# Adaptive-norm columns: four chunks before the first matmul instead of eight, and a gate that goes through DRAM

## The chip, the cores and the metric

One core of one Trainium2 chip runs the whole kernel in one launch. The metric is the device time in microseconds (us). The kernel before took 2486.54 us (median of 3 runs, 2486.16 to 2488.39). Engines: TensorE (PE) multiplies, VectorE (DVE) and ScalarE (ACT) work on vectors, SyncE (SP) issues all DMAs of the kernel before, and GpSimd (POOL) does nothing in it but four memsets.

## The reference

A sequence of 256 tokens of width 1024 (x, float32) goes through four layers of three sublayers: a gated feed-forward network (FFN), a mixer, and another FFN. Each sublayer is wrapped in an adaptive norm, whose shift, scale and gate come from one conditioning vector c:

```
mod = (silu(c) @ ada_w[l] + ada_b[l]).reshape(B, 3, 3, 1, D)      # 9 x 1024 numbers a layer
h   = rmsnorm(x, norm_g[l, j]) * (1 + mod[:, j, 1]) + mod[:, j, 0]
x   = x + 0.5 * (1 + mod[:, 0, 2]) * swiglu(h, wi, wo)            # FFN; in layers 2, 3 the gate has no "1 +"
x   = x + (1 + mod[:, 1, 2]) * mixer(h)
```

FFN: 1024 to 2 x 2816 to 1024. Mixers: a gated linear recurrence (hgrn) in layer 0, differential attention (diff) in layer 1, sparse attention beside a gated MLP (nsa) in layers 2 and 3. A last rmsnorm ends it. All in float32.

## The kernel before, in words

Twelve phases (l, j), l = 0..3 and j = 0..2, run one after the other. Weights come in pieces of 1 MB (128 x 2048), through a ring of three buffers `raw`. SP issues a piece when the piece three places earlier has been cut. "Cutting" splits it in a high and a low part, so that three float32r products make one float32 product: ACT copies the high part into `wH` (L461), DVE subtracts to get `wL` (L786), PE multiplies (L1371, L1373, L1375). Each engine's order is written out by hand, with counted semaphores; nothing is planned by a scheduler.

An FFN phase takes 33 pieces, in eleven turns: PE runs the up projection of 256 channels into `GU` (two pieces), ACT and DVE make silu(gate)*up, PE turns it (L1421), ACT and DVE split it (L524, L887), PE adds the down projection into `PY`.

The adaptive-norm numbers `mod` (288 columns of 128) are dot products on DVE. A chunk is four columns: two transfers of 1 MB of the transposed `ada_w` and four products of 128 x 1024 with `cond` (L793), then a small store (L813). Columns are in the order shift, scale, gate, eight each; so a phase's shift and scale are four chunks, and its gate two more. Of layer 0, eight chunks come ahead of everything (`start_products`, through a ring of five 1 MB buffers, L366), and ten in the turns of phase (0, 0); the later layers' chunks go one to a turn in FFN phases: 8 turns in each (l, 2), 10 in each (l, 0) (`ada_turns`).

At the boundary between phases (`boundary` on DVE, `norm` on ACT, `norm_and_first` on PE):

- DVE `columns` (L823 to L837) makes the gate column `gcol` and spreads it into `sh` (L833), and makes `scl`. PE `gate_broadcast` (L1378 to L1383) multiplies `sh` by the identity (16 matmuls) into `TM`, and ACT copies that to `gB` [128, 1024] (L511). `gB` is used at the next boundary, when DVE multiplies the phase's output with it (L841) and adds it to x (L845).
- For each of the two token tiles: ACT squares x (L473), DVE and ACT make the root (L818, L475, L821), DVE scales the identity (L861), PE multiplies x with it into `PY`, transposed (`turn_x`, L1389), DVE and ACT apply scale and shift (L868, L495), ACT and DVE split the result (L490, L874), PE starts the first products.
- In the very first boundary x is read straight after it has landed, and ACT does one more cut (the third piece) between the root of tile 0 and the split.

SP's order at the start: `cond`, `vec`, the identity, the first ten 1 MB transfers of `ada_w`, x, the other six, two weight pieces, six transfers of late constants (`late_constants`, L379 to L387, used first in hgrn), then the loop of phase (0, 0).

Of the kernel before, what the change touches and what calls it, by code (L numbers as in the profile page):

```python
# [25 lines left out]
P = 128  # L26
# [90 lines left out]
def build(nc, T, out, upto=99):  # L117

    with ExitStack() as ctx:
# [145 lines left out]
        s_gp = sem("s_gp")  # L265
# [50 lines left out]
        ADA_FIRST, ADA_REST = 8, 10  # L316
# [6 lines left out]
        def ada_turns(l, j):  # L323

            if j == 0:
                return l, ADA_FIRST, ADA_REST
            return (l + 1, 0, ADA_FIRST) if l + 1 < 4 else (l, 0, 0)

# [5 lines left out]
        def _(sp):  # L334
# [18 lines left out]
            def load_mixer(w, pieces):  # L353

                at = 0
                for k0, lo, width in pieces:
                    load(w[:, at:at + 4 * width], 4 * width)
                    at += 4 * width

            def load_start(c, q):  # L360

                n = t.next("start")
                slot = n % START_RING
                if n > START_RING:
                    sp.wait_ge(s_startfree, n - START_RING)
                sp.dma_start(start_[slot], T["ada_t"][0, 2 * c + q]).then_inc(s_start[slot], 16)  # L366
# [5 lines left out]
            def load_ada(l, c, q):  # L372
                v = T["ada_t"][l].rearrange("(c q) p n -> q p c n", q=2)
# [15 lines left out]
            def ffn(l, j):  # L389
                load_up(l, j, 0, 0)  # L390
                load_up(l, j, 0, 1)
                if (l, j) == (0, 0):
                    late_constants()
                if (l, j) == (1, 2):
                    sp.wait_ge(s_adafree, ADA_RING + 2 * (2 * ADA_REST + ADA_FIRST))
                    load_cond(1)
                la, c0, turns = ada_turns(l, j)

                def loop(first, count, with_ada):
                    with sp.Fori(0, count) as i:  # L400
                        t.enter(i, [(s_split, 3), ("piece", 3), (s_adafree, 2 * with_ada), ("ada", 2 * with_ada)])
                        load_up(l, j, first + i, 0)
                        if with_ada and (l, j) == (2, 2):
                            sp.wait_ge(s_x, NT * (3 * l + 2))
                        if with_ada:
                            load_ada(la, c0 + i, 0)
                        load_up(l, j, first + i, 1)
                        if with_ada:
                            load_ada(la, c0 + i, 1)
# [13 lines left out]
            for c in range(ADA_FIRST):  # L423
                for q in range(2):
                    load_start(c, q)
                if c == 4:
                    sp.dma_start(x[:, :, :], T["x"][0].rearrange("(t p) d -> p t d", p=P)).then_inc(s_in, 16)
            for l, j in PHASES:
                if j != 1:
                    ffn(l, j)  # L430
                elif l < 2:
                    load_mixer(T["ab"[l] + "_w"], (PIECES_A, PIECES_B)[l])
# [20 lines left out]
        def _(act):  # L453
# [23 lines left out]
            def norm(l, j):  # L477
# [48 lines left out]
            def ffn(l, j):  # L526
                norm(l, j)
                silu_gate()
                if (l, j) == (1, 2):
                    condition()  # L530

                def loop(count):
                    with act.Fori(0, count) as i:
                        t.enter(i, [("piece", 3), (s_eaten, 3), ("done", 3), (s_ht, 1)] + [(s, 32) for s in s_raw])
                        cut()
                        hidden_high()
                        cut()
# [5 lines left out]
                _, _, turns = ada_turns(l, j)  # L543
# [211 lines left out]
            condition()  # L755

# [17 lines left out]
        def _(dve):  # L774
# [14 lines left out]
            def products(l, q, piece, free):  # L789
# [7 lines left out]
            def start_products(q):  # L797
# [3 lines left out]
                products(0, q, start_[slot], s_startfree)  # L801

            def ada_products(l, q):
# [3 lines left out]
                products(l, q, ada[:, slot, :], s_adafree)  # L807

            def ada_store(l, c, free, count):

                dve.wait_ge(free, count)
                at = l * MODS + 4 * c
# [10 lines left out]
            def columns(l, j):  # L823

                m = (3 * l + j) * 3 * ND
                g = 2 * ND + (3 * l + j) * ND
                factor = 0.5 if j != 1 else 1.0
                gate = mod[:, m + 2 * ND:m + 3 * ND]
                if l < 2:
                    chained(dve.tensor_scalar(gcol[:, :], gate, 1.0, factor, ALU.add, ALU.mult))  # L830
                else:
                    chained(dve.tensor_scalar(gcol[:, :], gate, factor, None, ALU.mult))
                dve.tensor_copy(shf.rearrange("p (d n) -> p d n", n=P),  # L833
                                bc(gcol[:, :].unsqueeze(2), [P, ND, P])).then_inc(s_gcol, 1)
                dve.scalar_tensor_tensor(scl[:, :], mod[:, m + ND:m + 2 * ND], 1.0, cols[:, g:g + ND],
                                         ALU.add, ALU.mult).then_inc(s_scl, 1)
                dve.wait_ge(s_scl, t.next(s_scl))  # L837
# [8 lines left out]

            def boundary(l, j, pieces):
# [5 lines left out]
                if pieces:  # L853
                    dve.wait_ge(s_gb, t.next(s_gb))
# [3 lines left out]
                for i in range(NT):  # L858
                    toks = slice(i * P, (i + 1) * P)
                    root(i)  # L860
                    dve.tensor_scalar(diag[:, i, :], ident, rstd[:, i:i + 1], None, ALU.mult).then_inc(s_xn, 1)  # L861
# [28 lines left out]
            def ffn(l, j):  # L890
# [3 lines left out]
                la, c0, turns = ada_turns(l, j)  # L894

                def loop(count, with_ada):
                    with dve.Fori(0, count) as i:
# [5 lines left out]
                        if with_ada:  # L903
                            ada_products(la, 0)
                            ada_products(la, 1)
# [5 lines left out]
                        if with_ada:  # L911
                            ada_store(la, c0 + i, s_adafree, t.next(s_adafree, 0))
                    t.leave(count)

                if turns:
                    loop(turns, 1)
# [67 lines left out]
            def hgrn():  # L984
# [4 lines left out]
                for grp in range(2):  # L989
# [17 lines left out]
                    for n in range(9):  # L1007
# [5 lines left out]
                        if grp == 0 and n < 6 or grp == 1 and n == 7:  # L1013
                            cut()
                    select(8)
                    if grp == 1:
# [7 lines left out]
                                      ).then_inc(s_on, 1)  # L1024
                    d = slice(4 * grp, 4 * grp + 4)
# [302 lines left out]
            for c in range(ADA_FIRST):  # L1328
                start_products(0)
                start_products(1)  # L1330
                ada_store(0, c, s_startfree, 2 * c + 2)
            pieces = 0
            for n, (l, j) in enumerate(PHASES):
                if n == 0 or PHASES[n - 1][1] == 1:
                    cut()
                boundary(l, j, pieces)
                if j != 1:
# [8 lines left out]
            dve.wait_ge(s_gb, t.next(s_gb))  # L1346
# [6 lines left out]
            if len(PHASES) == 12:  # L1353
# [3 lines left out]
                for i in range(NT):  # L1357
                    root(i)
                    dve.scalar_tensor_tensor(x[:, i, :], x[:, i, :], rstd[:, i:i + 1], fg, ALU.mult, ALU.mult
                                             ).then_inc(s_x, 1)  # L1360


        @block.tensor
        def _(pe):
# [13 lines left out]
            def gate_broadcast():  # L1378
                pe.wait_ge(s_gcol, t.next(s_gcol))
                for d in range(ND):  # L1380
                    ins = pe.matmul(TM[:, d // 4, (d % 4) * P:(d % 4 + 1) * P], shf[:, d * P:(d + 1) * P], ident,
                                    start=True, stop=True)
                ins.then_inc(s_gp, 1)  # L1383

# [8 lines left out]
            def norm_and_first():  # L1393


                gate_broadcast()
# [15 lines left out]
                pe.wait_ge(s_gb, t.next(s_gb))  # L1412
# [459 lines left out]
```

## Time and profile before

| | before |
|---|---|
| median of 3 runs | 2486.54 us |
| the profiled execution | 2491.22 us, span 2489.6 us |
| PE / DVE / ACT busy | 91% / 66% / 44% |
| mean granted PE clock | 0.956 of full |
| DMA | 531.30 MB, 213 GB/s over the span |
| chain that ended last | PE 81%, DVE 9%, ACT 5%, issue 2%, DMA 2% |

The chain is followed back from the last instruction to whatever released each step. PE's share of it says that most of the time is matmuls back to back; the slice row of the page shows PE idle in the first slice (62 us) and the granted clock (PEclk) under full in some slices. A clock of 1.00 is 2.4 GHz, 0.5 is 1.2 GHz. A stretch that holds both levels shows a mean.

### The profile page before, as it was taken

Reading aid. Unit: us, or ns where it says so; the run is one execution under the profiler, and the core shown is the slowest. Engines: PE = TensorE matmul, PEld = TensorE weight load, DVE = VectorE, ACT = ScalarE, POOL = GpSimd, SP = SyncE. Lnnn points to the kernel's source line nnn. Section 1 sums busy time; section 2 is a strip of 40 time slices with the busy share of each in tenths; the row PEclk is TensorE's granted clock in tenths of the full one; section 3 lists DMA queues with packets and bytes.
Section 4 is the critical chain, followed back from the end, with each engine's and each line's share of the span. In section 5 each row is a group of like instructions: output and inputs, shape, how many; then the busy total and the mean of one; then the engine's idle time right before and its main releaser. Section 6 shows DMA issues by size and latency. Waiting matters only on the chain.

```text
span 2489.6 us, 30572 instructions
## 1 busy us (share of the span) xinstructions
PE 2273.3 (91%) x11004; PEld 1900.7 (76%) x11004; DVE 1654.5 (66%) x2245; ACT 1097.5 (44%) x1225; POOL 0.2 (0%) x4
## 2 busy tenths in 40 slices
PE   0999995899999997899999998999999999899998
PEld 0788884688788875788788787778878888777886
DVE  7677576677577776587577754468767776446444
ACT  1444543343444355434443444544344445464433
POOL 0000000000000000000000000000000000000000
PEclk9999997899999997999999997899999999799999
DMA  9687430388578731387588732348857883223553
GB/s 382 265 319 279 161 136 0 136 310 311 204 265 312 273 143 70 129 335 281 193 311 308 284 128 85 102 162 316 298 203 274 320 310 128 85 102 126 179 202 110
DMA packets 126426, 531.30 MB, mean 213 GB/s; under 512 B 14736, under 2 KB 15504, under 8 KB 107280
## 3 DMA queue, kind: packets, MB, share of 16 engines
q1 hardware_dynamic: 126352, 530.30, 58.8%
q8 instruction: 48, 0.79, 0.1%
q14 instruction: 26, 0.21, 0.0%
HBM read 529.19 MB, written 1.05 MB: 213 GB/s over the span
## 4 chain that ended last, share of the span: by engine, by line
PE 81%; DVE 9%; ACT 5%; issue 2%; DMA 2%; SPq 1%; DVEq 0%; ACTq 0%
PE GU L1371 14%; PE GU L1375 14%; PE GU L1373 14%; PE PY L1371 9%; PE PY L1373 9%; PE PY L1375 9%; DVE wL L786 2%; ACT wH L461 2%; PE PY L1389 2%; PE TM L1421 1%; DMA M<-in_ada_t 1%; PE GU L1758 1%; PE PY L1668 1%; DVE M L793 1%; DVE x L845 1%
## 5 line engine op out<-in xcount | busy, mean ns | idle before, releaser
L786 DVE TENSOR_TENSOR wL<-raw,wH 128x2048 fp32r<-128x2048 f32 x352 | 794.6, 2279 | 280.9 <-ACT wH L461 279.3
L461 ACT ACTIVATE wH<-raw 128x2048 fp32r<-128x2048 f32 x352 | 659.6, 1899 | 203.4 <-PE PY L1375 102.4
L1371 PE MATMUL GU<-wH,xH 128*128 128x512 f32 (+1 forms) x1600 | 635.2, 397 | 31.6 <-DVE xL L874 13.2
L1375 PE MATMUL GU<-wH,xL 128*128 128x512 f32 (+1 forms) x1600 | 623.8, 390 | 0.0
L1373 PE MATMUL GU<-wL,xH 128*128 128x512 f32 (+1 forms) x1600 | 623.3, 390 | 0.0
L1371 PEld LDWEIGHTS GU<-wH,xH 128*128 128x128 f32 x1600 | 302.8, 189 | 97.1 <-issue 32.6
L524 ACT ACTIVATE hH<-TM 128x512 fp32r<-128x512 f32 x88 | 52.7, 598 | 691.5 <-PE TM L1421 691.5
L1375 PEld LDWEIGHTS GU<-wH,xL 128*128 128x128 f32 x1600 | 302.3, 189 | 63.7
L1373 PEld LDWEIGHTS GU<-wL,xH 128*128 128x128 f32 x1600 | 303.0, 189 | 58.5
L793 DVE CUSTOM_DVE_ANT_0 ada<-ada,cond 128x1024 f32<-128x1024 f32 x256 | 298.0, 1220 | 0.0
L887 DVE TENSOR_TENSOR hL<-TM,hH 128x512 fp32r<-128x512 f32 x88 | 60.9, 691 | 253.8 <-ACT hH L524 253.7
L1371 PE MATMUL PY<-wH,hH 128*128 128x512 f32 x704 | 218.0, 391 | 12.5 <-DVE hL L887 12.4
L1373 PE MATMUL PY<-wL,hH 128*128 128x512 f32 x704 | 217.6, 390 | 0.0
L1375 PE MATMUL PY<-wH,hL 128*128 128x512 f32 x704 | 217.3, 390 | 0.0
L1371 PE MATMUL PY<-wH,xH 128*128 128x512 f32 x432 | 177.2, 410 | 8.2 <-DVE wL L786 6.8
L1373 PE MATMUL PY<-wL,xH 128*128 128x512 f32 x432 | 173.6, 402 | 0.0
L1375 PE MATMUL PY<-wH,xL 128*128 128x512 f32 x432 | 172.5, 399 | 0.0
L1371 PEld LDWEIGHTS PY<-wH,hH 128*128 128x128 f32 x704 | 131.7, 188 | 41.5 <-issue 10.3
L1375 PEld LDWEIGHTS PY<-wH,hL 128*128 128x128 f32 x704 | 132.7, 188 | 27.8
L1373 PEld LDWEIGHTS PY<-wL,hH 128*128 128x128 f32 x704 | 132.5, 188 | 27.7
L1371 PEld LDWEIGHTS PY<-wH,xH 128*128 128x128 f32 x432 | 84.8, 196 | 27.0 <-issue 5.5
L515 ACT ACTIVATE sh<-GU 128x512 f32<-128x512 f32 x88 | 52.7, 599 | 118.3 <-PE GU L1375 118.3
(275 smaller groups left out, 2013.9 us busy)
## 6 DMA issues: line engine op xcount, KB each, us to landing
raw<-in_up_w SPq DMA_DIRECT2D x352, 512.0 KB, 6.2
ada<-in_ada_t SPq DMA_DIRECT2D x128, 1024.0 KB, 8.1
raw<-in_down_w SPq DMA_DIRECT2D x176, 512.0 KB, 4.8
raw<-in_c_w SPq DMA_DIRECT2D x96, 512.0 KB, 4.3
raw<-in_a_w SPq DMA_DIRECT2D x40, 512.0 KB, 4.2
M<-in_ada_t SPq DMA_DIRECT2D x16, 1024.0 KB, 10.5
raw<-in_b_w SPq DMA_DIRECT2D x32, 512.0 KB, 4.3
M<-in_cmp_w SPq DMA_DIRECT2D x4, 1024.0 KB, 9.2
```

Of the source, the lines that this page charges most:

```text
L461: act.activation(wH[:, slot, 0:words], raw[:, slot, 0:words], ACT.Copy).then_inc(s_high, 1)
L515: act.activation(sh[:, 0, :, :], GU[:, :, 0:CF], ACT.Silu).then_inc(s_silu, 1)
L524: act.activation(hH[:, :, :].rearrange("p f s -> p (f s)"), TM[:, 0, :], ACT.Copy).then_inc(s_hh, 1)
L786: dve.tensor_tensor(wL[:, slot, 0:words], raw[:, slot, 0:words], wH[:, slot, 0:words], ALU.subtract).then_inc(s_split, 1)
L793: ins = dve.tensor_tensor_reduce(w, w, cond[:, :], 1.0, 0.0, ALU.mult, ALU.add, acc[:, 2 * q + b:2 * q + b + 1])
L845: dve.tensor_tensor(x[:, i, :], x[:, i, :], xn[:, i, :], ALU.add).then_inc(s_x, 1)
L887: dve.tensor_tensor(hL[:, :, :].rearrange("p f s -> p (f s)"), TM[:, 0, :], hH[:, :, :].rearrange("p f s -> p (f s)"), ALU.subtract).then_ ...
L1371: pe.matmul(outs[i], aH, wh[i], start=first, stop=False)
L1373: pe.matmul(outs[i], aH, wl[i], start=False, stop=False)
L1375: ins = pe.matmul(outs[i], aL, wh[i], start=False, stop=last)
L1389: ins = pe.matmul(PT[:, i, d, :], x[:, i, d * P:(d + 1) * P], diag[:, i, :], start=True, stop=True)
L1421: ins = pe.transpose(TM[:, 0, f * S + i * P:f * S + (i + 1) * P], sh[:, 1, i, f * P:(f + 1) * P], ident)
```

## The change

- `ADA_FIRST` is 4: four chunks ahead of the first phase. The turns of (0, 0) take chunks 4 to 13, hgrn takes chunks 14 and 15 (one in each head group, in DVE's order), (0, 2) takes 16 to 25 in ten turns. From (1, 0) on all is as it was.
- x is loaded after the second chunk. ACT squares both tiles of x straight after `cond`, and DVE does root and scaled identity of tile 0 after the third chunk, of tile 1 after the fourth.
- The late constants are loaded after the ten turns of (0, 0).
- `gate_broadcast`, the spread of `gcol` and ACT's copy to `gB` are gone. DVE makes `gcol` a little later (in (0, 0) and (0, 2) after two turns); GpSimd's queue writes it to a DRAM scratch of 12 x 1024, waits for it and for x of the boundary before, and reads it back into all 128 partitions of `gB`.

```diff
-        ADA_FIRST, ADA_REST = 8, 10
+        ADA_FIRST = 4
+        MIXER_CHUNKS = (14, 15)
...
+            if l == 0:
+                return (ADA_FIRST, 10) if j == 0 else (16, 10)
             if j == 0:
-                return l, ADA_FIRST, ADA_REST
-            return (l + 1, 0, ADA_FIRST) if l + 1 < 4 else (l, 0, 0)
+                return 18 * l + 8, 10
+            return 18 * l + 18, 8 if l < 3 else 0
...
# SP
+                    if n in chunks:          # hgrn: {10: 14, 16: 15}
+                        load_ada(chunks[n], 0)
+                        load_ada(chunks[n], 1)
                     load(w[:, at:at + 4 * width], 4 * width)
...
-                if (l, j) == (0, 0):
-                    late_constants()
...
                 if turns:
                     loop(1, turns, 1)
+                if (l, j) == (0, 0):
+                    late_constants()
...
-                if c == 4:
+                if c == 1:
                     sp.dma_start(x[:, :, :], ...)
# ACT
-                root_table()
+                if not first:
+                    root_table()
...
-                    root(i, (l, j) == PHASES[0])
+                    if not first:
+                        root(i)
...
-                act.wait_ge(s_gp, t.next(s_gp))
-                act.activation(gB[:, :], TMf, ACT.Copy).then_inc(s_gb, 1)
...
             condition()
+            for i in range(NT):
+                root(i, True)
# DVE
-                dve.tensor_copy(shf.rearrange("p (d n) -> p d n", n=P),
-                                bc(gcol[:, :].unsqueeze(2), [P, ND, P])).then_inc(s_gcol, 1)
...
-                if turns:
-                    loop(turns, 1)
+                if l == 0:
+                    loop(2, 1)
+                    gate_column(l, j)
+                    c0 = c0 + 2
+                    loop(turns - 2, 1)
...
+                        if grp == 0 and n == 4:
+                            mixer_chunk(MIXER_CHUNKS[0])
...
+                    if grp == 1:
+                        mixer_chunk(MIXER_CHUNKS[1])     # after s_on
...
             for c in range(ADA_FIRST):
                 start_products(0)
                 start_products(1)
-                ada_store(0, c, s_startfree, 2 * c + 2)
+                ada_store(c, s_startfree, 2 * c + 2)
+                if c > 1:
+                    root(c - 2)
+                    scaled_identity(c - 2)
# GpSimd
+            for n in range(len(PHASES)):
+                pool.wait_ge(s_gcol, n + 1)
+                pool.dma_start(T["gates"][n].rearrange("(d p) -> p d", p=P), gcol[:, :],
+                               allow_slow_non_contiguous=True).then_inc(s_gd, 16)
+                pool.wait_ge(s_gd, 16 * (n + 1))
+                if n:
+                    pool.wait_ge(s_x, NT * n)
+                pool.dma_start(gB[:, :], T["gates"][n:n + 1].broadcast_to([P, D])).then_inc(s_gb, 16)
# PE
-                gate_broadcast()
                 turn_x(0)
...
-                pe.wait_ge(s_gb, t.next(s_gb))
```

## Rows read from the trace of the kernel before

**Rows 1.** The page's head: span, and busy time of each engine

```profile
span 2489.6 us, 30572 instructions
PE 2273.3 (91%) x11004; PEld 1900.7 (76%) x11004; DVE 1654.5 (66%) x2245; ACT 1097.5 (44%) x1225; POOL 0.2 (0%) x4
```

**Rows 2.** Stretches: start:end, length, busy by engine, PEclk, DMA share, GB/s

```profile
10.00:20.00 10.00, 0.00 (x0) 0.00 (x0) 9.86 (x19) 0.00 (x0) 0.00 (x0) 1.00 1.01 424
123.40:140.20 16.80, 16.80 (x78) 13.90 (x77) 12.73 (x14) 6.61 (x5) 0.00 (x0) 1.00 0.94 326
639.70:656.50 16.80, 16.80 (x79) 13.90 (x78) 8.08 (x5) 6.61 (x5) 0.00 (x0) 1.00 0.53 187
```

**Rows 3.** Timeline of the start: start, duration, engine, instruction [idle before, releaser]

```profile
9.11 1.22 DVE L793 CUSTOM_DVE_ANT_0 M<-M,cond 128x1024 f32<-128x1024 f32 x1 [8.24 <-DMA M<-in_ada_t]
...
28.98 1.22 DVE L793 CUSTOM_DVE_ANT_0 M<-M,cond 128x1024 f32<-128x1024 f32 x1
...
36.49 1.23 DVE L793 CUSTOM_DVE_ANT_0 M<-M,cond 128x1024 f32<-128x1024 f32 x1 [2.57 <-DMA M<-in_ada_t]
...
42.40 2.22 SPq L385 DMA_DIRECT2D vb<-in_a_onorm  x1
...
51.45 0.16 DVE L813 TENSOR_TENSOR mod<-acc,vec 128x4 f32<-128x4 f32 x1
...
59.02 0.15 DVE L818 TENSOR_SCALAR st<-st 128x1 f32<-128x1 f32 x1
...
59.63 0.28 DVE L861 TENSOR_SCALAR M<-cst,rstd 128x128 f32<-128x128 f32 x1
...
64.27 1.91 ACT L461 ACTIVATE wH<-raw 128x2048 fp32r<-128x2048 f32 x1 [4.87 <-DMA raw<-in_up_w]
...
67.09 0.77 PE L1371 MATMUL GU<-wH,xH 128*128 128x512 f32 x1 [3.92 <-DVE xL L874]
```

**Rows 4.** Timeline of hgrn, around the places of chunks 14 and 15

```profile
325.95 3.78 PE L1523 MATMUL TM<-M 128*128 128x128 f32 x16 [5.24 <-DVE M L968]
...
355.06 0.69 DVE L949 TENSOR_TENSOR M<-M 128x512 f32<-128x512 f32 x1
...
358.12 1.95 PE L1523 MATMUL TM<-M 128*128 128x128 f32 x16
...
460.44 1.23 DVE L937 TENSOR_TENSOR xL<-GU,xH 128x1024 fp32r<-128x1024 f32 x1 [6.46 <-ACT xH L574]
```

**Rows 5.** Timeline of the boundaries after (0, 0) and after hgrn

```profile
255.24 2.29 DVE L786 TENSOR_TENSOR wL<-raw,wH 128x2048 fp32r<-128x2048 f32 x1 [0.30 <-ACT wH L461]
...
259.77 1.95 PE L1381 MATMUL TM<-cst,sh 128*128 128x128 f32 x16
262.17 2.05 PE L1389 MATMUL PY<-M,x 128*128 128x128 f32 x16 [0.46 <-DVE M L861]
...
263.44 1.37 DVE L868 TENSOR_SCALAR M<-PY,scl,mod 128x128 f32<-128x128 f32 x4 [0.19 <-PE PY L1389]
265.29 0.47 PE L1371 MATMUL GU<-wH,xH 128*128 128x512 f32 x1 [1.06 <-DVE xL L874]
...
474.22 2.29 DVE L786 TENSOR_TENSOR wL<-raw,wH 128x2048 fp32r<-128x2048 f32 x1 [4.40 <-ACT wH L461]
...
477.38 1.95 PE L1381 MATMUL TM<-cst,sh 128*128 128x128 f32 x16
481.14 2.21 PE L1389 MATMUL PY<-M,x 128*128 128x128 f32 x12 [1.81 <-DVE M L861]
```

**Rows 6.** Stretches around idle time of PE, columns as in rows 2

```profile
325.20:332.00 6.80, 6.05 (x23) 5.52 (x24) 6.14 (x8) 3.17 (x3) 0.00 (x0) 0.52 0.48 171
482.20:485.60 3.40, 3.16 (x13) 2.73 (x13) 1.92 (x7) 1.94 (x6) 0.00 (x0) 0.53 0.30 118
666.50:669.90 3.40, 1.90 (x11) 1.44 (x10) 1.58 (x4) 1.63 (x2) 0.00 (x0) 1.00 0.98 310
1663.20:1666.60 3.40, 2.34 (x12) 1.86 (x11) 2.88 (x8) 2.99 (x9) 0.00 (x0) 1.00 0.00 0
```

**Rows 7.** DMA issues: out<-in, engine, count, KB each, median us to landing

```profile
raw<-in_up_w SPq DMA_DIRECT2D x352, 512.0 KB, 6.2
```

More of the change, by code:

```diff
@@ L264, in build @@
         s_gcol = sem("s_gcol")
-        s_gp = sem("s_gp")
+        s_gd = sem("s_gd")
         s_gb = sem("s_gb")
@@ L351, in load_down, with load_mixer @@
                 load(T["down_w"][l, j // 2][bass.ds(c, 1)].rearrange("c p n -> p (c n)"))
-            def load_mixer(w, pieces):
+            def load_mixer(w, pieces, chunks={}):
                 at = 0
-                for k0, lo, width in pieces:
+                for n, (k0, lo, width) in enumerate(pieces):
+                    if n in chunks:
+                        load_ada(chunks[n], 0)
+                        load_ada(chunks[n], 1)
                     load(w[:, at:at + 4 * width], 4 * width)
@@ L365, in load_start, with load_ada @@
                     sp.wait_ge(s_startfree, n - START_RING)
-                sp.dma_start(start_[slot], T["ada_t"][0, 2 * c + q]).then_inc(s_start[slot], 16)
+                sp.dma_start(start_[slot], T["ada_t"][2 * c + q]).then_inc(s_start[slot], 16)
             def load_cond(k):
                 sp.dma_start(cond[:, :], T["cond"][k:k + 1, :].broadcast_to([P, D])).then_inc(s_cond, 16)
-            def load_ada(l, c, q):
-                v = T["ada_t"][l].rearrange("(c q) p n -> q p c n", q=2)
+            def load_ada(c, q):
+                v = T["ada_t"].rearrange("(c q) p n -> q p c n", q=2)
                 slot = t.next("ada") % ADA_RING
@@ L391, in ffn @@
                 load_up(l, j, 0, 1)
-                if (l, j) == (0, 0):
-                    late_constants()
                 if (l, j) == (1, 2):
-                    sp.wait_ge(s_adafree, ADA_RING + 2 * (2 * ADA_REST + ADA_FIRST))
+                    sp.wait_ge(s_adafree, ADA_RING + 2 * 32)
                     load_cond(1)
-                la, c0, turns = ada_turns(l, j)
+                c0, turns = ada_turns(l, j)
                 def loop(first, count, with_ada):
@@ L405, in loop @@
                         if with_ada:
-                            load_ada(la, c0 + i, 0)
+                            load_ada(c0 + i, 0)
                         load_up(l, j, first + i, 1)
                         if with_ada:
-                            load_ada(la, c0 + i, 1)
+                            load_ada(c0 + i, 1)
                         load_down(l, j, first + i - 1)
@@ L431, in _ @@
                 elif l < 2:
-                    load_mixer(T["ab"[l] + "_w"], (PIECES_A, PIECES_B)[l])
+                    load_mixer(T["ab"[l] + "_w"], (PIECES_A, PIECES_B)[l], ({10: 14, 16: 15}, {})[l])
                 else:
@@ L480, in norm @@
                 m = (3 * l + j) * 3 * ND
-                root_table()
+                first = (l, j) == PHASES[0]
+                if not first:
+                    root_table()
                 act.wait_ge(s_scl, t.next(s_scl))
                 for i in range(NT):
-                    root(i, (l, j) == PHASES[0])
+                    if not first:
+                        root(i)
                     if i == 0:
@@ L541, in loop @@
                     t.leave(count)
-                _, _, turns = ada_turns(l, j)
+                _, turns = ada_turns(l, j)
                 if turns:
@@ L787, in cut, with products @@
                                   ALU.subtract).then_inc(s_split, 1)
-            def products(l, q, piece, free):
+            def products(q, piece, free):
                 for b in range(2):
@@ L800, in start_products, with ada_products, ada_store @@
                 dve.wait_ge(s_start[slot], t.next(s_start[slot], 16))
-                products(0, q, start_[slot], s_startfree)
-            def ada_products(l, q):
+                products(q, start_[slot], s_startfree)
+            def ada_products(q):
                 slot = t.next("ada") % ADA_RING
                 dve.wait_ge(s_ada[slot], t.next(s_ada[slot], 16))
-                products(l, q, ada[:, slot, :], s_adafree)
-            def ada_store(l, c, free, count):
+                products(q, ada[:, slot, :], s_adafree)
+            def ada_store(c, free, count):
                 dve.wait_ge(free, count)
-                at = l * MODS + 4 * c
+                at = 4 * c
                 chained(dve.tensor_tensor(mod[:, bass.ds(at, 4)], acc[:, :], bT[:, bass.ds(at, 4)], ALU.add))
@@ L826, in columns, with gate_column @@
                 g = 2 * ND + (3 * l + j) * ND
+                dve.scalar_tensor_tensor(scl[:, :], mod[:, m + ND:m + 2 * ND], 1.0, cols[:, g:g + ND],
+                                         ALU.add, ALU.mult).then_inc(s_scl, 1)
+                dve.wait_ge(s_scl, t.next(s_scl))
+            def gate_column(l, j):
+                m = (3 * l + j) * 3 * ND
                 factor = 0.5 if j != 1 else 1.0
@@ L829, in columns, with mixer_chunk @@
                 if l < 2:
-                    chained(dve.tensor_scalar(gcol[:, :], gate, 1.0, factor, ALU.add, ALU.mult))
+                    dve.tensor_scalar(gcol[:, :], gate, 1.0, factor, ALU.add, ALU.mult).then_inc(s_gcol, 1)
                 else:
-                    chained(dve.tensor_scalar(gcol[:, :], gate, factor, None, ALU.mult))
-                dve.tensor_copy(shf.rearrange("p (d n) -> p d n", n=P),
-                                bc(gcol[:, :].unsqueeze(2), [P, ND, P])).then_inc(s_gcol, 1)
-                dve.scalar_tensor_tensor(scl[:, :], mod[:, m + ND:m + 2 * ND], 1.0, cols[:, g:g + ND],
-                                         ALU.add, ALU.mult).then_inc(s_scl, 1)
-                dve.wait_ge(s_scl, t.next(s_scl))
+                    dve.tensor_scalar(gcol[:, :], gate, factor, None, ALU.mult).then_inc(s_gcol, 1)
+            def mixer_chunk(c):
+                ada_products(0)
+                ada_products(1)
+                ada_store(c, s_adafree, t.next(s_adafree, 2))
             def gated_output(i):
@@ L845, in add_output, with scaled_identity @@
                 dve.tensor_tensor(x[:, i, :], x[:, i, :], xn[:, i, :], ALU.add).then_inc(s_x, 1)
+            def scaled_identity(i):
+                dve.tensor_scalar(diag[:, i, :], ident, rstd[:, i:i + 1], None, ALU.mult).then_inc(s_xn, 1)
             def boundary(l, j, pieces):
@@ L853, in boundary @@
                 if pieces:
-                    dve.wait_ge(s_gb, t.next(s_gb))
+                    dve.wait_ge(s_gb, t.next(s_gb, 16))
                     dve.wait_ge(s_y, t.next(s_y))
@@ L859, in boundary @@
                     toks = slice(i * P, (i + 1) * P)
-                    root(i)
-                    dve.tensor_scalar(diag[:, i, :], ident, rstd[:, i:i + 1], None, ALU.mult).then_inc(s_xn, 1)
+                    if pieces:
+                        root(i)
+                        scaled_identity(i)
                     if pieces and i == 0:
@@ L893, in ffn @@
                     dve.wait_ge(s_cs, 2)
-                la, c0, turns = ada_turns(l, j)
+                c0, turns = ada_turns(l, j)
                 def loop(count, with_ada):
@@ L903, in loop @@
                         if with_ada:
-                            ada_products(la, 0)
-                            ada_products(la, 1)
+                            ada_products(0)
+                            ada_products(1)
                             t.next(s_adafree, 2)
@@ L911, in loop @@
                         if with_ada:
-                            ada_store(la, c0 + i, s_adafree, t.next(s_adafree, 0))
+                            ada_store(c0 + i, s_adafree, t.next(s_adafree, 0))
                     t.leave(count)
-                if turns:
-                    loop(turns, 1)
+                if l == 0:
[3 more added lines that the diff above has]
+                    loop(turns - 2, 1)
+                else:
+                    gate_column(l, j)
+                    if turns:
+                        loop(turns, 1)
                 if turns < NF - 1:
@@ L1336, in _ @@
                 boundary(l, j, pieces)
+                if j == 1:
+                    gate_column(l, j)
                 if j != 1:
@@ L1345, in _ @@
                 pieces = 3 * NF if j != 1 else PIECES[l] - (22 if l > 1 else 0)
-            dve.wait_ge(s_gb, t.next(s_gb))
+            dve.wait_ge(s_gb, t.next(s_gb, 16))
             dve.wait_ge(s_y, t.next(s_y))
@@ L1360, in _ @@
                                              ).then_inc(s_x, 1)
+        @block.gpsimd
+        def _(pool):
+            for n in range(len(PHASES)):
[6 more added lines that the diff above has]
+                pool.dma_start(gB[:, :], T["gates"][n:n + 1].broadcast_to([P, D])).then_inc(s_gb, 16)
         @block.tensor
@@ L1376, in times_three @@
                 return ins
[L1378 to L1383, printed above, removed]
             def turn_x(i):
```

3 lines of the change are left out of this document (2 added, 1 removed).

## The prediction

> **What bounds the kernel now.** I read the page's head first: PE is busy for 91% of 2489.6 us, DVE for 66% [rows 1]. Then the stretches of one FFN turn. With a chunk of four products on DVE a turn takes 16.80 us and PE is busy in all of it; without one it takes 16.80 us too, DVE falling from 12.73 to 8.08 us [rows 2]. So in the 88 turns PE is the bound, and chunks there are free. What can be won lies where PE waits: the start, where it does its first product of weights at 67.09 us [rows 3]; the recurrence of layer 0 (hgrn); the eleven boundaries. Last I read the granted clock after each such wait.
>
> **The start.** DVE takes its first chunk at 9.11 us and the fifth at 28.98, 4.97 us each. x was queued after the fifth chunk and made DVE wait 2.57 us at 36.49. The eighth chunk is stored at 51.61. The third weight piece stands behind the late constants in SP's queue and starts ACT's cut only at 64.27, after 4.87 us of waiting [rows 3]. The transfers run at 424 GB/s [rows 2], so one of 1.05 MB takes 2.5 us, the same as the half chunk that DVE makes of it: DVE and the transfers go in step.
>
> After the change, forward from 9.11:
> - two chunks, 9.94 us: 19.1. Then x (the wait of 2.57, moved here): 21.6. Third chunk: 26.6. Root and scaled identity, 0.9 us (59.02 to 59.91 [rows 3]): 27.5. Fourth chunk: 32.5.
> - ACT stands in the root of tile 1 until DVE comes to it, so its first cut starts at 32.9 at the earliest. By then the piece is there: at 36.49 twelve transfers of 1 MB had landed (eleven half chunks and x) [rows 3], and in the new order the twelfth is the third weight piece (eight, x, three). Two cuts of 1.91 us: 34.8 and 36.7.
> - DVE cuts from 35.0, makes `scl`, cuts again from 37.4 (2.29 us each as at 255.24 [rows 5]): 39.7. ACT makes the third cut meanwhile (37.4 to 39.3), for which the piece lands at about 36.5.
> - The transposed x has been waiting in `PY` since 30 us or so. From DVE's first scaling to the first matmul it is 1.85 us (263.44 to 265.29 [rows 5]): 41.6.
>
> That is 25.5 us before 67.09. Four chunks alone are 19.9 of it; the rest is the third piece, which no longer waits behind the late constants, and the root, gone from the chain. Bounds: 28 if the wait for x is shorter, 21 if the third piece lands later, since the ada transfers behind it now share the queue. The first matmuls ran at half clock before and will again, so that cancels. Late constants: six issues, 42.40 to 48.88 with what stands between [rows 3]; at the end of (0, 0) they hold up the last piece of that phase by at most 8 us. A piece is issued when the third before it is cut, with three pieces to a turn 11 us and more before ACT wants it, and needs 6.2 to land [rows 7]: 8 + 6.2 - 11 = 3 us late at ACT, which is busy for 6.61 of 16.80 us there [rows 2]: 0, at worst 3.
>
> **Hgrn.** Chunk 14 goes in front of the DVE group at 355.06. Its four instructions, one every 0.6 us, the last 0.69 long, end at 357.55 and make the operands of PE's matmuls at 358.12, which stand there without idle time before them [rows 4]: 0.6 us to spare. 4.97 less 0.6 is 4.4 us of PE standing still. After that DVE is in step again, PE is the bound to the group's end, and no wait takes the 4.4 back: +4.4. Chunk 15 comes after DVE has handed over its last result at 454.0 (460.44 less the 6.46 us that it then idles [rows 4]), and 4.97 + 0.2 fit in: 0. If they didn't fit, it would cost up to 5. The two more turns with a chunk in (0, 2) cost 0 by rows 2.
>
> **The gate.** DVE loses the copy of 0.69 and PE the 16 matmuls. Neither was on the path: behind the copy DVE still waited for ACT's cut, 0.30 us at 255.24 and 4.40 at 474.22; PE waited 0.46 and 1.81 us for the scaled identity after the gate's matmuls [rows 5]. ACT's copy of 1.03 us ends while PE is busy with tile 1. Gain 0. The gate column, now behind the boundary, puts 0.2 us in front of the chain of differential attention: +0.2. GpSimd's two transfers have a whole phase to land, 180 us or more; a read of 512 KB at 424 GB/s is 1.2 us. The write goes in 1024 elements of four bytes, which no row here shows from this queue; it starts from nothing lost, and it costs only if it delays weight pieces by more than the 6.2 us that lie between landing and use. I take 0; bounds 0 and 1 us per gate.
>
> **What the removed matmuls did.** They filled PE's wait. After the seven FFN ends PE now idles from 259.77 to 262.17, 2.4 us where 0.46 was; after the four mixers from 477.38 to 481.14, 3.76 where 1.81 was [rows 5]. What such idling does to the clock: 1.5 us idle inside 666.5 to 669.9 and the clock stays at 1.00 (every FFN turn's end is so, but one); 1.81 us before 481.14, and the next 3.4 us are at 0.53, that is 1.2 GHz nearly throughout; the same 1.81 before 1661, and the clock stays at 1.00 [rows 6]. Of four mixer ends three fell. 5.24 us before 325.95 [rows 4], and 6.8 us ran at 0.52 [rows 6]. So 2.4 us lies on the falling side of the nearest rows: I take a fall in 7 of 10. A fall of 3.4 us costs 1.7 if PE is busy throughout; part of it lies in the 1.06 us of waiting before 265.29, and some falls last longer: 1.4. FFN ends: 7 x 0.7 x 1.4 = +6.9. Mixer ends: the fourth falls too and some last longer: +2. The 4.4 us hole in hgrn is most like the row of 5.24, where 6.05 us of busy PE at half speed lost 3.0: +2.5. Bounds of the whole clock term: 0 and +22 (all eleven at 1.7 and hgrn at 3.0).
>
> The Trainium skill (page TensorE: Matmul & The Clock Gate, section "HAM oscillation — how this bites in real kernels") lets the clock fall only after idle gaps longer than those that arise at the FFN ends. By it they would cost nothing and the sum would be 6.9 us lower; the trace disagrees already, as 481.14 with its 1.81 us shows.
>
> **Sum.** -25.5 + 4.4 + 0.2 + 6.9 + 2 + 2.5 = -9.5. The profiled execution took 2491.2, so 2481.7; the median of the runs is 4.7 us under it, so 2477.0. A difference of 0.2% (5 us) is what a measurement tells from no change here: under 2481.6 is faster.
>
> **Rivals.**
> - *The clock doesn't care at the FFN ends.* For it: 666.5 and 1663.2, where 1.5 and 1.81 us did nothing. Against: 481.14. Without the 6.9: 2470.1. If mixers and hgrn don't care either, 2465.6. (The first is the page's rule above.) 0.22.
> - *The start is bound by the queue.* The weight pieces now come close behind the chunks, and ACT, which does nothing for 25 us in the root of tile 1, cuts them late. If the third piece lands 5 us later than I have it (the wait before 64.27 was 4.87) and DVE's first cut slips too, the start gives 19 instead of 25.5: 2483.5. Against: SP issues the pieces from about 17 us on, with nothing but chunks in front. 0.1.
> - *Slower: the clock stays down at every boundary.* One mechanism: without the gate's matmuls the low clock at each of the eleven boundaries lasts as long as after 325.20, 6.8 us, and costs 3.0. Then 11 x 3.0 = 33 stands for the 8.9: 2501.1. It decides from 1.7 us a boundary on, where (25.5 - 7.1) / 11 is used up. Against: at 482.2 the clock was back after one short stretch, since PE has work as soon as x is there. 0.04.
> - *The gate comes late or disturbs.* If four-byte writes hold up the pieces at twelve places by 1 us past their slack, +12: 2489. 0.04. For it: 1024 elements are as many small packets as two whole weight transfers have rows. The Trainium skill (DMA: Bandwidth & Descriptors, the table's row on a strided last dim) has one descriptor per element here; no run shows yet what that costs, and the sum doesn't rest on it.
>
> **Chances.** My forecast 0.6 (its own range 2471 to 2482.5, from the start's 21 to 28 and the clock's chance), the rivals 0.22, 0.1, 0.04, 0.04. Faster: 0.57 of the forecast's 0.6, the whole 0.22, 0.04 of the second: 0.83. Slower: 0.04 and a little of the fourth: 0.05. The rest, 0.12, within 0.2%. The range of 8 in 10 goes from the first rival's lower value to the second's: 2465.5 to 2484.
>
> **What would show it.** The first L1371 near 41.6 us, ACT's first cut near 33, idle PE of 4.4 us in front of the sixth group of L1523-type matmuls; chunk 15 inside DVE's idle time; turns at 16.80 us still; 2.4 and 3.8 us of idle PE in front of the turning of x, with a clock near 0.5 behind most of them, and a mean clock under 0.956. I am wrong if the first matmul is past 46 us, if the clock holds at 1.00 at the FFN ends, or if ACT's cuts in FFN turns begin to wait for weight pieces after the gate's transfers.

## The result: slower by 0.4%

| | median us | lowest to highest | profiled run, its span, mean clock |
|---|---|---|---|
| before, 5 runs | 2486.54 | 2483.68 to 2490.78 | 2491.22, 2489.6, 0.956 |
| after, 5 runs | 2497.99 | 2492.82 to 2500.01 | 2495.44, 2493.7, 0.950 |

After to before is 1.004, 95% interval 1.0028 to 1.0052. The forecast was 2477.0. Measured again beside other kernels the changed kernel took 2498.0 (1.0042, 1.0029 to 1.0055).

The medians differ by 11.5 us, but the two profiles by only 4.1: the profiled run of before lies 4.7 us over its median, that of after 2.6 under. What follows accounts for the 4.1. For the other 7 us there is only a hint, the mean granted clock: 0.949 in the median of the twelve later runs of after, 0.958 in the twenty of before beside them, while the two profiles have 0.950 and 0.956.

The start did what was forecast. In the timeline of after, ACT's first cut and the first product of weights (start, duration, engine, line, instruction, idle time before and its end), against [rows 3]:

```profile
21.16 1.23 DVE L800 CUSTOM_DVE_ANT_0 M<-M,cond 128x1024 f32<-128x1024 f32 x1 [2.57 <-DMA M<-in_ada_t]
...
32.17 3.69 ACT L466 ACTIVATE wH<-raw 128x2048 fp32r<-128x2048 f32 x2
...
40.55 0.77 PE L1420 MATMUL GU<-wH,xH 128*128 128x512 f32 x1 [9.58 <-DVE xL L894]
```

So 67.09 became 40.55, and 26.5 us were won. Where were more than 26.5 given back? I measured each phase between two products that every FFN has: the first turning of the hidden tile and the last one. Lengths in us, worked out from the starts of these products in the two profiles:

```
                    first at   inside the eight FFNs, in order                        between them, in order
before                89.5     162.6 162.6 162.6 163.0 162.6 162.6 162.6 162.6       252.9 33.2 192.0 33.2 270.2 33.2 265.7
after                 62.7     163.6 164.6 165.2 166.0 166.1 165.2 165.4 162.6       261.5 34.1 193.9 35.6 264.4 33.8 270.4
after - before       -26.8      +1.0  +2.0  +2.6  +3.0  +3.5  +2.6  +2.8   0          +8.6 +0.9  +1.9 +2.4  -5.8 +0.6  +4.7
```

The FFNs sum to +17.5, hgrn's stretch is +8.6, the three FFN-to-FFN boundaries +3.9, the other three mixers together +0.8: with the start +4.0, of the 4.1 by which the spans differ. In each of the seven FFNs all of the excess lies in one turn, which starts 22 to 25 us after the gate column's write went out; that turn takes 17.8 to 20.3 us where [rows 2] had 16.80. The eighth FFN has no ada chunks, and its write cost nothing.

GpSimd's timeline in the FFN of (1, 0), then SP's, and below them the stretches of the same kernel (start:end, length, busy by engine, PEclk, DMA share, GB/s):

```profile
681.18 0.90 POOL L1404 DMA_DIRECT2D gates<-gcol  x1 [154.38 <-DVE gcol L844]
691.68 0.56 POOL L1409 DMA_DIRECT2D gB<-gates  x1 [9.61 <-DMA gates<-gcol]
```

```profile
678.16 0.85 SPq L345 DMA_DIRECT2D raw<-in_up_w  x2
686.68 0.33 SPq L381 DMA_DIRECT2D ada<-in_ada_t  x1
687.26 0.85 SPq L345 DMA_DIRECT2D raw<-in_up_w  x2
```

```profile
682.00:684.00 2.00, 2.00 (x11) 1.62 (x10) 2.00 (x1) 0.00 (x0) 0.08 (x1) 1.00 0.51 115
684.00:686.00 2.00, 2.00 (x11) 1.65 (x10) 2.00 (x4) 0.00 (x0) 0.00 (x0) 1.00 0.00 0
686.00:688.00 2.00, 2.00 (x12) 1.70 (x11) 2.00 (x5) 0.92 (x2) 0.00 (x0) 1.00 0.00 0
688.00:690.00 2.00, 2.00 (x10) 1.64 (x10) 1.87 (x4) 2.00 (x2) 0.00 (x0) 1.00 1.45 49
690.00:692.00 2.00, 2.00 (x11) 1.65 (x10) 2.00 (x2) 1.29 (x1) 0.32 (x1) 1.00 0.33 49
692.00:694.00 2.00, 2.00 (x11) 1.65 (x10) 2.00 (x2) 0.60 (x1) 0.25 (x1) 1.00 0.51 168
```

The zeros from 684 to 688 are not the write's doing: SP had issued nothing since 678.16, and the kernel before, which has no such write, is at zero from 682 to 690 in the same way. The stop shows behind it. From 688 to 692 the core moves 49 GB/s, for the weights too, whose transfers are in another queue; the pieces issued at 687.26, 691.99 and 694.21 take 11.5, 12.9 and 13.2 us to land. In the first FFN, where the write goes out at 88.45 and SP issues a piece at 93.54, it is the same:

```profile
92.00:94.00 2.00, 2.00 (x10) 1.67 (x9) 2.00 (x5) 0.00 (x0) 0.00 (x0) 1.00 1.15 221
94.00:96.00 2.00, 2.00 (x10) 1.65 (x10) 1.06 (x2) 0.00 (x0) 0.00 (x0) 1.00 0.28 10
96.00:98.00 2.00, 2.00 (x13) 1.65 (x12) 0.41 (x1) 1.04 (x2) 0.00 (x0) 1.00 1.04 59
98.00:100.00 2.00, 2.00 (x11) 1.62 (x10) 0.89 (x2) 1.46 (x2) 0.07 (x1) 1.00 0.62 49
```

In the FFN of (1, 0) ACT, and behind it DVE, then wait for the piece (ACT's and DVE's timelines, the page's DMA issues, then the list of waits: us in total, times, longest):

```profile
700.00 1.92 ACT L466 ACTIVATE wH<-raw 128x2048 fp32r<-128x2048 f32 x1 [6.85 <-DMA raw<-in_up_w]
```

```profile
701.95 2.29 DVE L793 TENSOR_TENSOR wL<-raw,wH 128x2048 fp32r<-128x2048 f32 x1 [7.27 <-ACT wH L466]
```

```profile
gates<-gcol POOLq DMA_DIRECT2D x12, 4.0 KB, 10.4
```

```profile
POOL gB L1409 <- DMA gates<-gcol: 121.0, 12, 11.8
ACT wH L466 <- DMA raw<-in_up_w: 93.7, 31, 7.6
```

Before, ACT waited 66.3 us for in_up_w, 44.9 of it in one wait at the start. 4 KB take 10.4 us from issue to landing, more than the 6.2 of 512 KB in [rows 7].

Hgrn has its hole, and the clock falls behind it (timeline, then stretches; the first answers to [rows 6] at 325.20, the others to the FFN and mixer ends there):

```profile
336.83 2.50 PE L1563 MATMUL TM<-M 128*128 128x128 f32 x10 [4.23 <-DVE M L995]
```

```profile
334.80:341.60 6.80, 4.77 (x22) 4.77 (x23) 6.23 (x8) 5.94 (x5) 0.00 (x0) 0.54 1.01 419
236.70:240.10 3.40, 3.37 (x16) 3.18 (x15) 2.29 (x6) 1.33 (x2) 0.00 (x0) 0.54 0.00 0
461.40:468.20 6.80, 4.81 (x19) 4.35 (x20) 3.53 (x10) 4.40 (x9) 0.00 (x0) 0.52 0.42 170
862.00:865.40 3.40, 2.34 (x18) 2.09 (x18) 2.70 (x7) 2.60 (x6) 0.00 (x0) 1.00 0.00 0
```

Read so around each boundary, the granted clock fell to 1.2 GHz at five of seven FFN ends (none before) and at two of four mixer ends (three before). The group of the products that turn x shows the idle time behind it; 27.2 of its 57.4 us stand at the start and 30.2 at the eleven boundaries:

```profile
L1431 PE MATMUL PY<-M,x 128*128 128x128 f32 x384 | 58.8, 317 | 57.4 <-DVE M L864 57.0
```

The same group of before had 297 ns a product and 10.9 us of idle time, all at the boundaries.

### The profile page after: what moved, and what is told of

The parts are those of the page before. It is cut to its first block, busy times and chain, and to the rows that moved or that the text cites. A ratio compares the mean times of both kernels' runs of the same rounds, so it can differ in the third digit from the quotient of the medians.

```text
span 2493.7 us, 30211 instructions
## 1 busy us (share of the span) xinstructions
PE 2267.6 (91%) x10812; PEld 1886.9 (76%) x10812; DVE 1644.8 (66%) x2233; ACT 1089.8 (44%) x1212; POOL 17.9 (1%) x28
## 4 chain that ended last, share of the span: by engine, by line
PE 71%; DVE 12%; ACT 6%; DMA 6%; issue 4%; SPq 1%; DVEq 0%; ACTq 0%
PE GU L1420 11%; PE GU L1424 11%; PE GU L1422 11%; PE PY L1420 9%; PE PY L1422 9%; PE PY L1424 8%; DMA raw<-in_up_w 4%; ACT wH L466 3%; DVE wL L793 3%; DVE ada L800 2%; PE PY L1431 2%; PE TM L1461 1%; DMA raw<-in_c_w 1%; PE PY L1611 1%; PE PY L1708 1%
## 5 line engine op out<-in xcount | busy, mean ns | idle before, releaser
L800 DVE CUSTOM_DVE_ANT_0 ada<-ada,cond 128x1024 f32<-128x1024 f32 x272 | 316.6, 1220 | 0.0
L1431 PE MATMUL PY<-M,x 128*128 128x128 f32 x384 | 58.8, 317 | 57.4 <-DVE M L864 57.0
L1420 PEld LDWEIGHTS PY<-wH,xH 128*128 128x128 f32 x432 | 85.2, 197 | 27.2 <-issue 5.8
```

What stands on the lines that cost most here:

```text
L800: ins = dve.tensor_tensor_reduce(w, w, cond[:, :], 1.0, 0.0, ALU.mult, ALU.add, acc[:, 2 * q + b:2 * q + b + 1])
L1420: pe.matmul(outs[i], aH, wh[i], start=first, stop=False)
L1431: ins = pe.matmul(PT[:, i, d, :], x[:, i, d * P:(d + 1) * P], diag[:, i, :], start=True, stop=True)
```

## The experiments

Theory W: the write of single elements stops the weights' transfers. Rivals: C, PE idles where its gate products stood, and its clock falls; R, the 512 KB read holds the weights up; S, the gate costs nothing and the moved chunks give the start's gain back. Ratios are to the kernel before, run beside each. The edits are told in short, + for what was added, - for what was removed.

**The gate's matmuls back (`pe_gate`).** In the changed kernel:

```
 BY_DRAM = [(0, 0), (0, 2)]         # the other ten as before:
+columns():  gcol, then tensor_copy(shf, gcol spread)
+PE:         8 x matmul(TM, shf, ident) ahead of turn_x(0)
+ACT:        activation(gB, TMf, Copy)
```

> The changed kernel, with the gate made by PE and ACT as in the kernel before in the ten phases in which its column is there at the boundary; the first two FFNs, whose gate chunk comes later, keep the DRAM way. Theory W: the start's 26.8 us are kept, the hgrn phase costs 8.4 us and two gates 3.1 us: 2486.5 - 26.8 + 8.4 + 3.1 = 2471, at most 2475. Rival C: the same within 3 us (PE's products are back), so this run does not part W from C. Rival S: near the changed kernel, 2490 to 2498.

Measured 2473.59, 0.9949 (0.9935 to 0.9964). S falls: with its start and its chunks the change is worth 13 us. The five later FFNs are back at 162.6 and 163.0 us; the two that keep the DRAM way have 165.5 and 165.0.

**The column in runs of 128 bytes (`runs`).**

```
+dve.transpose(gT, gcol32)                       # 32x32 blocks
-pool.dma_start(gates[n] "(d p) -> p d", gcol)   # 1024 elements
+for b in range(4): pool.dma_start(gates[n] "(d b i) -> b d i"[b], gT[32*b:32*b+8])
```

> The changed kernel with one thing altered: the gate column is turned by a 32x32 transpose on DVE and written in 32 runs of 128 bytes (4 transfers) and not in 1024 elements of four bytes; the 512 KB read, its queue and its time stay. Theory W: the 17.8 us of the seven FFN turns and most of the mixers' part go: 2476 to 2482. Rival R (the 512 KB read holds the weights up, not the write): 2496 to 2498. Rival C: 2496 to 2498. Rival S: 2496 to 2498.

Measured 2479.2, 0.9964 (0.9953 to 0.9976), 18.8 under the changed kernel. All FFNs are back at the 162.6 and 163.0 us of before, while the read of 512 KB still stands in the first turn: R falls, W stands. The piece issued at 682.50, in the place of the one at 687.26 above, lands after 7.2 us where that took 11.5. The same stretch of GpSimd, and its waits:

```profile
676.65 2.04 POOL L1409 DMA_DIRECT2D gates<-gT  x4 [157.57 <-DVE gT L849]
680.01 0.55 POOL L1414 DMA_DIRECT2D gB<-gates  x1 [1.32 <-DMA gates<-gT]
```

```profile
POOL gB L1414 <- DMA gates<-gT: 29.9, 12, 4.8
ACT wH L468 <- DMA raw<-in_up_w: 23.5, 13, 3.7
```

**Products ahead of the turn of x (`warm`).**

```
+pe.wait_ge(s_scl, ...); for d in range(8): pe.matmul(TM[...], ident, ident)
 turn_x(0)
```

> The changed kernel with eight 128x128 products of the identity on PE ahead of each phase's turn of x, into a bank that nobody reads, where the kernel before had its gate's products. Theory W: what the clock gives, less what eight products take: 2491 to 2497. Rival C: the longer low-clock time goes, 2486 to 2489. Rival S: 2498.

Measured 2487.31, 1.0006 (0.9996 to 1.0016), 10.7 under the changed kernel, though the write still costs its 0.9 to 3.6 us a turn here. The time is the one that I had given W's rival C (2486 to 2489), and after `runs` both hold: it is a second cause beside W. No FFN end falls now and one mixer end does; the eight products take 1.95 us, and the trace counts each twice. The end of (0, 0) and the group of the turn of x:

```profile
237.00:240.40 3.40, 2.34 (x19) 2.09 (x18) 2.69 (x7) 2.60 (x7) 0.00 (x0) 1.00 0.00 0
```

```profile
L1431 PE MATMUL PY<-M,x 128*128 128x128 f32 x384 | 50.3, 286 | 11.1 <-DVE M L864 11.0
```

**The gate's way alone (`gate_only_2`), and the write alone (`write_only`), in the kernel before.**

```
 columns():   gcol ahead of the norm, as before;  -tensor_copy, -PE products, -ACT copy
+POOL:        write gates[n] <- gcol; read gB <- gates[n]        (write_only: the write alone, nothing removed)
```

> The kernel before, with nothing of the change but the gate's way: column to DRAM by GpSimd's queue in 1024 elements of four bytes, back by one 512 KB read, the PE products and the ACT copy gone; chunks, start and waits are those of before. By the runs so far the write costs 19 us (2498.0 - 2479.2) and the missing PE products 10.7 us (2498.0 - 2487.3). If both terms are the gate's alone, they stand here too: 2486.5 + 19 + 10.7 = 2516, 2510 to 2518. If the missing products cost only where the write also delays the phase (a shared term): 2505. Rival S, by which the gate costs nothing on the old chunk plan: 2486.5.

> The kernel before with 12 added writes of the gate column to a DRAM scratch that nobody reads, in 1024 elements of four bytes each, on GpSimd's queue, issued when the column is there; everything else stays, PE's products too. If the write alone holds the weights up: +15 to +25 us, 2502 to 2511 (here it falls at the boundary, where more may wait for the weights than in mid-phase). If it is the 512 KB read or PE's clock that costs: within 2 us of before, 2485 to 2489.

Measured 2499.6, 1.0052 (1.0037 to 1.0068), and 2494.2, 1.0032 (1.002 to 1.0044). Both miss: 13.6 and 8.2 us, not 30 and 15 to 25. In both all FFNs are at 162.6 and 163.0 us, as before, although each of the twelve writes takes 11.4 and 12.1 us to land. What shows is the start, 5.6 and 4.3 us later by the first turning. In `gate_only_2` the first write goes out at 56.5 us, and the third piece lands 5.4 us later than before (timeline of ACT, 64.27 in [rows 3]):

```profile
69.67 1.91 ACT L461 ACTIVATE wH<-raw 128x2048 fp32r<-128x2048 f32 x1 [10.43 <-DMA raw<-in_up_w]
```

The rest of the 13.6 is not traced (its profile is 6.5 us longer than before's). The profile of `write_only` is 7.7 us longer, and what the start leaves of it lies in the last mixer's stretch and has no shown cause. What W had missed: in these kernels the column goes out ahead of the norm, in the changed one behind it. Hence the next.

**The same write, earlier (`early`).** The changed kernel:

```
 columns():  +if (l, j) not in ((0, 0), (0, 2)): wait for s_gd of the last; gate column here
 ffn()/mixers: -gate_column(l, j) in those ten phases
```

> The changed kernel, the gate column still written in 1024 elements of four bytes, but in ten phases computed and sent ahead of the norm, where PE waits and the weights' ring is full, and not behind it in the first hidden turn; only the first two FFNs, whose gate chunk comes later, keep their place. If the place of the write decides (its stop of some 8 us is covered at the boundary, not in a turn): the excess of the five FFN turns goes, 2.6 + 3.0 + 3.5 + 2.6 + 2.8 = 14.5 us, so 2498.0 - 14.5 = 2483.5, 2480 to 2486. If only its form decides: 2496 to 2500.

Measured 2480.88, 0.9973 (0.9961 to 0.9985). The place decides: the two FFNs that keep theirs take 163.8 and 165.1 us, the others 162.6 and 163.0. The write is the slow one still (12.0 us to land in the median), and hides: GpSimd's read now waits for x and not for it (GpSimd's timeline, and the stretch behind it):

```profile
656.15 0.90 POOL L1411 DMA_DIRECT2D gates<-gcol  x1 [128.31 <-DVE gcol L851]
670.86 0.56 POOL L1416 DMA_DIRECT2D gB<-gates  x1 [13.80 <-DVE x L867]
```

```profile
660.80:662.80 2.00, 0.85 (x4) 0.38 (x2) 0.85 (x1) 1.06 (x2) 0.00 (x0) 1.00 1.72 283
662.80:664.80 2.00, 0.91 (x5) 0.92 (x6) 1.57 (x4) 1.78 (x3) 0.00 (x0) 0.81 1.09 61
664.80:666.80 2.00, 2.00 (x11) 2.00 (x11) 1.01 (x4) 0.39 (x2) 0.00 (x0) 0.50 0.65 72
```

**Fewer single elements (`half`: 512, `elem128`: 128; the rest of the column in runs).**

> The changed kernel with half of the column (512 elements) written as single elements and the other half in 16 runs of 128 bytes. If the stop grows with the number of elements, it is some 4 to 5 us and the ring covers it: all FFN turns 16.8 us, 2479 to 2483. If any write of single elements costs the same, whatever their number: 2496 to 2500.

> The changed kernel with 128 of the column's values written as single elements and the other 896 in 28 runs of 128 bytes. With 1024 single elements the column's write took 10.4 us to land and with 512 it stopped the weights' transfers as long (8.8 us waited for it, against 8.7 to 11.8), so the stop has not been seen to grow with the count. If it grows with the count at all, 128 elements (an eighth) cost little: the FFN turns are 16.8 us and the time 2479 to 2483. If the stop is there with any such write, 2496 to 2505.

Measured 2504.37, 1.0068 (1.0054 to 1.0082), and 2494.43, 1.003 (1.0016 to 1.0043). The expectation that the price shrinks with the count is wrong: an eighth of the elements gives back only 3.6 of the 18.8 us. GpSimd waits a tenth less with half and a fifth less with an eighth, and in both the last five FFNs with chunks take 2.8 to 6.1 us more than before (the first two 1.0 or less). Half of them even cost 6.4 us more than all, for which I have no shown cause; both versions send five transfers for one. The waits of `half`, then of `elem128`:

```profile
POOL gB L1416 <- DMA gates<-gcol: 109.0, 12, 11.3
ACT wH L468 <- DMA raw<-in_up_w: 93.9, 25, 9.5
```

```profile
POOL gB L1416 <- DMA gates<-gcol: 95.4, 12, 9.2
ACT wH L468 <- DMA raw<-in_up_w: 86.2, 27, 8.3
```

So the price hangs on there being such a write more than on its size. What in it makes the stop (elements of four bytes, or one from each of 128 partitions, where the runs come from 32) these kernels don't part.

**Chunk 14 elsewhere (`c14`), and the changed kernel again.**

```
-if grp == 0 and n == 4: mixer_chunk(MIXER_CHUNKS[0])
+if grp == 0: mixer_chunk(MIXER_CHUNKS[0])     # ahead of select(8)
```

> The changed kernel with chunk 14 moved within the hgrn mixer: from behind DVE's work on level 4 of the first head group, where PE waits 4.2 us for DVE and then runs 6.8 us at the low clock, to the place ahead of the last level's selection, where DVE was idle for 5.4 us. If PE's wait is the chunk's: -4 to -7 us against the changed kernel, 2491 to 2494. If DVE's idle time there is needed after all (the chunk is late and the head norm behind it waits): 2498 to 2500.

> The changed kernel once more, beside these runs. Its time should be 2498.0 within 3 us, as measured. The move of chunk 14 alone came out 12.2 us lower than that (2485.8), 7.1 us of it in the hgrn phase by the two profiles; if the changed kernel now is near 2493, that difference was partly one of when it was run.

Measured 2485.81, 1.0001 (0.9986 to 1.0016), and 2498.0. Hgrn's stretch went from 261.5 to 254.4 us, and PE has no idle time where it had 4.23. That is 7.1 of the 12.2; the rest isn't in the profiles, whose spans differ by 2.1 us only, so the move is shown for 7 us, the upper end of what was expected, and no more.

**Put together (`best`, `best_early`, `best24`).** The changed kernel with `runs`, `warm` and `c14`; the same with the column sent early; that with 24 products for eight.

> The changed kernel with three parts altered together: the gate column written in 32 runs of 128 bytes, eight products of the identity on PE ahead of the turn of x, chunk 14 ahead of the last level's selection. If the three terms add up: 2498.0 - 18.8 (write) - 10.7 (products) - 5 (chunk) = 2463.5, 2460 to 2467. If the clock term was bound to the write's delays: 2471 to 2476.

> The version with runs of 128 bytes, eight products ahead of the turn of x and chunk 14 moved (2467.4 so far), with the gate column sent ahead of the norm in ten phases as well. Nothing is left there for the place to save (all FFN turns are 16.8 us): 2467.4 within 2 us. If the 512 KB read, which comes earlier too, meets the weights of the first turn less: up to 2 us lower.

> The fastest version so far (2460.95) with 24 products ahead of each turn of x in place of 8. If PE's clock still falls at phase starts for want of work before the turn of x (low-clock time is 200 us in that version, 205 with the products in the changed kernel), more of it goes: 2455 to 2460. If what is left of low clock lies inside the mixers, or the added products delay the turn of x: 2460 to 2464.

Measured 2467.4, 0.9925 (0.9911 to 0.9938); 2460.95, 0.9895 (0.9878 to 0.9912); 2490.94, 1.0017 (1.0006 to 1.0028). The three terms don't quite add up (30.6 of 41.7 us). `best_early` is the fastest, 37 us under the changed kernel; its last 6.5 us lie in three mixers' stretches (8.5 us shorter by the profiles), for which I have no shown cause; two profiles of the changed kernel differ by 4 us in such a stretch. 24 products are too many: they take 5.5 us, and the three short stretches go from 33.2 to about 36 (PE in `best24`):

```profile
655.57 5.52 PE L1452 MATMUL TM<-cst 128*128 128x128 f32 x48
660.92 1.95 PE L1443 MATMUL PY<-M,x 128*128 128x128 f32 x16
```

## Why the prediction was wrong

- *Start, -25.5.* Right: 26.5 by the first matmul, 26.8 by the first turning. ACT's cut came at 32.17 (32.9 forecast).
- *Hgrn, +4.4 and +2.5 for its clock.* Right: a hole of 4.23 us, then 6.8 us at 0.54. With one FFN end (1.0) and a mixer's (0.5) I had 8.4 for that stretch; it is 8.6. Chunk 15 cost nothing that shows.
- *Clock, FFN ends +6.9 and mixer ends +2.* Right in kind: 2.2 us of idle time (2.4 forecast), a fall at five of seven (0.7 each forecast). The three FFN-to-FFN stretches gave +3.9 for 2.9. Of the mixer ends two fell and not four; the three stretches came to +0.8, where the same terms give +4.5. That says little: in the profile of the changed kernel taken again the last two of them take 268.6 and 266.1 us, where the table has 264.4 and 270.4. `warm` puts the lost products at 10.7 us by medians, with 8.9 in the sum.
- *The gate's transfers, 0.* This is the step that failed. I wrote "I take 0; bounds 0 and 1 us per gate"; in the profile it is 17.5 us, 2.5 a turn in seven turns, and 18.8 by the medians of `runs`. With this one thing mended the kernel took 2479.2, 2.2 over the forecast. I had seen that the write has 1024 elements of four bytes and that no row shows one, and still gave it no price: the bound of 1 us had no row behind it.
- *The slack of 6.2 us.* It was the right thing to hold against the write, but the number was misread. In [rows 7] 6.2 us is the time from issue to landing, not from landing to use. In the trace of before the tightest piece of a turn, issued at 748.53, lands after 6.5 us and is cut at 757.84, so 2.8 us are left to it. Behind the write pieces took 11.5 to 13.2 us to land.
- *The rival "the gate comes late or disturbs", 0.04.* It had the right mechanism with too small a size, 1 us at twelve places for 2.5 at seven, and too small a chance. Its sentence on the rows is wrong too: a transfer of 512 KB has 128 rows of 4 KB, so 1024 elements are as many as the rows of eight, and the queue rows of `write_only` count 32 packets to a write. The Trainium skill (DMA: Bandwidth & Descriptors, "Rules for kernel authors", the row on a strided last dim) says of this form of transfer that it becomes one descriptor per element, and advises a contiguous last dim. `runs` bears the advice out with its 18.8 us; the price does not go by the number of elements (128 cost nearly as much).
- *"It starts from nothing lost."* Wrong too, and it hid the second half. The moved column took the write from the boundary, where PE waits and the ring is full, into the turns of an FFN with chunks, where the weights and the chunks need 326 GB/s [rows 2] and there is little slack. `early` undoes only that and wins 17 us.

The sum was -9.5 and the profiles say +4.1. Without the gate's 17.5 it would be -13.4; by its own profile `runs` has -10.0. The forecast also took 4.7 us off for the profiled run of before, which sat above its median. After's profile sat under its own, so the 7 us between +4.1 and the measured +11.5 stay open. The last test that I had named, ACT's cuts waiting for weight pieces behind the gate's transfers, was the one that came true.

## What to carry to other kernels

A transfer of single elements is to be priced by a measured transfer of its kind, not by its bytes; where the trace has none, the bound is an open one, times the number of places, and a test of it comes first. Ask at which moment of the ring it is issued, since the same write cost nothing that shows at the boundaries between FFNs (33.1 to 33.2 us in `write_only`) but 2.5 us in a turn. And work that an idle engine does for nothing may keep its clock up: before it is taken away, count the idle time that is left.

## What the runs showed of the hardware

- A write of 1024 single elements of four bytes (4 KB) on GpSimd's queue took 10.4 us to land. Beside it the whole core moved 10 to 59 GB/s for 6 us (94 to 100 us in after), and pieces issued in the other queue landed after 11.5 to 13.2 us. With 128 such elements the FFN turns lost as much (2.8 to 4.1 us in five of them). Beside four transfers of 8 runs of 128 bytes a piece in the same place landed after 7.2 us.
- Eight products of 128x128, 1.95 us, ahead of the turn of x kept the granted clock at 1.00 at all seven FFN ends; without them PE stood idle for 2.2 us, and it fell to 0.5 at five.
